# Depthwise convolution of a two-layer decoder step: four channel chunks on TensorE in sixteen 32x32 pieces, four on VectorE with prompt and sample taps in turn

## The reference, cut to what matters

```python
def conv_glu(h, w_pw1, b_pw1):
    u = h @ w_pw1 + b_pw1
    a, g = jnp.split(u, 2, axis=-1)
    return a * jax.nn.sigmoid(g)

def conv_rest(u_ext, w_dw, b_dw, ln_g, ln_b, w_pw2, b_pw2):
    c = lax.conv_general_dilated(u_ext, w_dw[:, None, :], window_strides=(1,), padding='VALID',
                                 dimension_numbers=('NWC', 'WIO', 'NWC'),
                                 feature_group_count=D_CONV) + b_dw
    c = layernorm(c, ln_g, ln_b)
    return jax.nn.silu(c) @ w_pw2 + b_pw2
```

## Time and profile before

| | us |
|---|---|
| median of three runs | 2173.63 (2168.54 to 2174.45) |
| profiled execution, its own time | 2175.05 |
| its span in the trace | 2173.3 |
| first product starts (L1968) | 1257.4 |
| last gate (gate 7) starts | 1442.7 |
| diagonal matmuls end | 1475.4 |
| second product starts | 1500.5 |
| expert layer 1 starts its matmuls | 1632.8 |

### The profile page before, as it was taken

The page is one execution under the profiler, slowest core; times in us unless marked ns, Lnnn a source line. Parts: engine busy times, 40 slices in busy tenths (PEclk is TensorE's granted clock), DMA queues, the critical chain, the costliest instruction groups (busy, mean ns, idle before and its releaser), DMA issues.

```text
span 2173.3 us, 32073 instructions
## 1 busy us (share of the span) xinstructions
PE 1667.7 (77%) x12540; PEld 806.9 (37%) x12540; DVE 688.0 (32%) x1216; ACT 303.1 (14%) x716; POOL 291.4 (13%) x416
## 2 busy tenths in 40 slices
PE   4999888887885778778777296768849778887770
PEld 2444455554445222223223174544443222222220
DVE  3214477767215100000000369983160000000003
ACT  1000344343210000000000100003101000000001
POOL 1001113212100100000000065400010000000001
PEclk9999989898895899999999698889959989889995
DMA  9476389889821699999999589902308999999973
GB/s 360 149 270 223 130 304 345 320 330 338 342 111 49 253 427 429 427 416 428 422 417 421 195 296 328 320 11 116 132 32 331 427 426 424 422 426 426 428 333 144
DMA packets 98431, 659.02 MB, mean 303 GB/s; under 512 B 14939, under 2 KB 14940, under 8 KB 69498
## 3 DMA queue, kind: packets, MB, share of 16 engines
q1 hardware_dynamic: 67450, 557.96, 64.1%
q0 software_dynamic: 30864, 99.45, 12.5%
HBM read 643.07 MB, written 96.53 MB: 340 GB/s over the span
## 4 chain that ended last, share of the span: by engine, by line
PE 42%; DMA 35%; DVE 16%; issue 4%; ACT 2%; SPq 1%; POOL 0%; DVEq 0%; POOLq 0%; ACTq 0%
DMA ring<-in 32%; PE ps L1861 13%; PE ps L1548 9%; DVE big L1446 7%; PE ps L1823 6%; PE ps L1505 3%; PE ps L1667 2%; PE ps L1989 1%; DVE ring L1052 1%; DMA big<-y_rows 1%; PE ps L1877 1%; PE ps L1607 1%; PE ps L1652 1%; PE ps L1583 1%; PE ps L1968 1%
## 5 line engine op out<-in xcount | busy, mean ns | idle before, releaser
L1861 PE MATMUL ps<-ring,big 128*32 128x512 f32 (+1 forms) x2816 | 511.7, 657 | 153.2 <-DMA ring<-in 150.4
L1861 PEld LDWEIGHTS ps<-ring,big 128*32 128x32 f32 (+1 forms) x2816 | 161.0, 133 | 502.9 <-issue 431.1
L1246 DVE TENSOR_TENSOR big<-big,ps 128x512 f32<-128x512 f32 x32 | 22.0, 687 | 892.3 <-PE ps L1861 892.3
L1877 PE MATMUL ps<-ring,big 128*32 128x512 f32 (+1 forms) x1408 | 230.0, 602 | 37.9 <-ACT big L634 23.0
L1548 PE MATMUL ps<-ring,act_t 128*128 128x512 f32 (+1 forms) x480 | 189.5, 594 | 1.2 <-DVEq L320 1.2
L634 ACT ACTIVATE big<-ps 128x512 f32<-128x512 f32 (+2 forms) x128 | 71.3, 557 | 748.5 <-PE ps L1505 433.7
L1505 PE MATMUL ps<-cst,big 128*128 128x128 f32 (+2 forms) x552 | 85.9, 310 | 109.2 <-DVE big L1019 68.8
L1968 PE MATMUL ps<-act_t,ring 128*128 128x288 f32 x512 | 133.1, 424 | 36.5 <-DVE big L1431 35.3
L1446 DVE SCALAR_TENSOR_TENSOR big<-big,par 128x512 f32<-128x512 f32 x150 | 152.3, 1015 | 5.1
L1877 PEld LDWEIGHTS ps<-ring,big 128*32 128x32 f32 (+1 forms) x1408 | 72.7, 123 | 172.8 <-issue 172.8
L1823 PE MATMUL ps<-ring,big 128*128 128x512 f32 (+1 forms) x288 | 121.7, 608 | 8.0 <-ACT big L954 7.1
(11 more groups left out here) (262 smaller groups left out, 1497.5 us busy)
## 6 DMA issues: line engine op xcount, KB each, us to landing
ring<-in SPq DMA_DIRECT2D x206, 2048.0 KB, 19.3
out<-in SPq DMA_DIRECT2D x16, 4080.0 KB
ring<-in SPq DMA_DIRECT2D x128, 256.0 KB, 7.8
ring<-in POOLq DMA_DIRECT2D x128, 256.0 KB, 8.4
ring<-in SPq DMA_DIRECT2D x24, 512.0 KB, 5.3
ring<-in POOLq DMA_DIRECT2D x24, 512.0 KB, 4.5
ring<-in SPq DMA_DIRECT2D x8, 1024.0 KB, 8.7
ring<-in POOLq DMA_DIRECT2D x8, 1024.0 KB, 7.7
```

The lines of the kernel that those rows point to most:

```text
L1246: V.tensor_tensor(hb, sg, ps[:, 1, :], ALU.mult).then_inc(m["hb"], 1)
L1861: ins = mm(ps[half, i, :], XgT[:, par_, k, half], slot(eslots(w)[i], 8)[:, k, :], start=(k == 0), stop=(k == KC - 1))
L1877: ins = mm(ps[half, 5 + h, :], hbT[:, k, half], slot(eslots(w)[2], 4)[:, k, h * 512:(h + 1) * 512], start=(k == 0), stop=(k == 3))
```

## The change

- TensorE takes four chunks (4 to 7) in sixteen pieces a step; VectorE takes chunks 0 to 3.
- VectorE does each prompt tap and the same tap of the 64 sample columns in turn; each waits for the one two places back, that is for the one before of its own kind. The samples of chunks 4 to 7 are done by `sample_taps`.
- GpSimd does no taps and no diagonals: VectorE builds the diagonals ahead of gate 0, in slot 1.
- The gates stand at other places. The turned samples and products move to slot 2.
- `w_pw2` goes to slots 0 and 3. Slot 0 is loaded at once behind `w_pw1`; slot 3 after chunk 3, and the window copies stand behind that wait. The experts' first loads go in the order 5, 2, 4, 1, 0, 3.
- Reciprocal, scaling and Silu are done for 288 columns of all chunks and then for the other 288; `project` waits for the second half at its third unit.

The core of the diff:

```diff
     def moe_base(l, s):
-        return 16 + (16 if s in (2, 3) else 0) + l * (16 * NPB + 16)
+        return 16 + (16 if s in (2, 3) else 0) + l * (16 * NPB + 16 + {1: -16, 3: 16}.get(s, 0))
...
-    D_CH = KC - 3
-    diag = slot(2, 128)
-    fresh = ring[:, 3, 0:KC * TS].rearrange("p (c q) -> p c q", c=KC)
+    D_CH = KC - 4
+    diag = slot(1, 128)
+    fresh = ring[:, 2, 0:KC * TS].rearrange("p (c q) -> p c q", c=KC)
...
-            for s in ((5, 4, 0, 2, 3, 1) if l == 0 else (2, 5, 3, 0, 4, 1)):
+            for s in ((5, 4, 0, 2, 3, 1) if l == 0 else (5, 2, 4, 1, 0, 3)):
...
-                    if s < 2:
-                        sp.wait_ge(p_mm, len(P_UNITS) + (5, len(P_UNITS))[s])
+                    if s in (0, 3):
+                        sp.wait_ge(p_mm, len(P_UNITS) + (5 if s == 0 else len(P_UNITS)))
+                    elif s == 2:
+                        sp.wait_ge(pw_mm, KC + 1)
+                        sp.wait_ge(ln_steps, 1)
                     else:
-
-                        sp.wait_ge(pw_mm, KC + 2 if s == 2 else KC)
-                        if s == 3:
-                            sp.wait_ge(ln_steps, 1)
+                        sp.wait_ge(pw_mm, KC + 2 if s == 1 else KC)
...
-        sp.wait_ge(pw_mm, 1)
-        for n in range(2):
-            sp.dma_start(slot(n, 8), w2[n]).then_inc(loaded[n], 16)
+        sp.dma_start(slot(0, 8), w2[0]).then_inc(loaded[0], 16)
+        sp.wait_ge(pw_mm, 4)
+        sp.dma_start(slot(3, 8), w2[1]).then_inc(loaded[3], 16)
         for i in range(6, 2 * NB):
             copy_window(i)
...
         for ch in range(KC):
             act.wait_ge(ln_steps, KC + 4 + ch)
-            A_(cc[:, ch, :], cc[:, ch, :], ACT.Silu, bias=PR("ln_b")[:, ch:ch + 1],
+            A_(cc[:, ch, 0:HALF], cc[:, ch, 0:HALF], ACT.Silu, bias=PR("ln_b")[:, ch:ch + 1],
                scale=PR("ln_g")[:, ch:ch + 1]).then_inc(ln_squares, 1)
+        for ch in range(KC):
+            act.wait_ge(ln_steps, 2 * KC + 4 + ch)
+            ins = A_(cc[:, ch, HALF:], cc[:, ch, HALF:], ACT.Silu, bias=PR("ln_b")[:, ch:ch + 1],
+                     scale=PR("ln_g")[:, ch:ch + 1])
+        ins.then_inc(ln_squares, 1)
...
-            o = cc[:, ch, 0:TP]
             for j in range(CK):
                 if j in gates:
                     gate(gates[j])
-                i = u_ext[:, ch, j:j + TP]
-                if j == 0:
-                    link(V.tensor_scalar(o, i, wdw[:, ch, 0:1], PR("b_dw")[:, ch:ch + 1], ALU.mult, ALU.add))
-                else:
-                    link(V.scalar_tensor_tensor(o, i, wdw[:, ch, j:j + 1], o, ALU.mult, ALU.add))
+                for o, i in ((cc[:, ch, 0:TP], u_ext[:, ch, j:j + TP]), (sample_sums(ch), us[:, ch, :, j:j + NQ])):
+                    if j == 0:
+                        S(V.tensor_scalar(o, i, wdw[:, ch, 0:1], PR("b_dw")[:, ch:ch + 1], ALU.mult, ALU.add))
+                    else:
+                        dve.wait_ge(dve_step, S.n - (3 if j in gates else 1))
+                        S(V.scalar_tensor_tensor(o, i, wdw[:, ch, j:j + 1], o, ALU.mult, ALU.add))
...
+        for a in range(4):
+            V.tensor_tensor(diag[:, 32 * a:32 * a + CK, :], C("eye32").unsqueeze(1).broadcast_to((P, CK, 32)),
+                            wdw[:, D_CH + a, :].unsqueeze(2).broadcast_to((P, CK, 32)), ALU.mult)
+        for a in range(4):
+            ins = V.tensor_tensor(diag[:, 32 * a + CK, :], C("eye32"),
+                                  PR("b_dw")[:, D_CH + a:D_CH + a + 1].broadcast_to((P, 32)), ALU.mult)
+        ins.then_inc(diagonals, 1)
         gate(0)
-        taps(0, {22: 1})
-        taps(1, {13: 2})
-        taps(2, {4: 3, 26: 4})
-        taps(3, {17: 5})
-        taps(4, {8: 6, 30: 7})
+        taps(0, {16: 1})
+        taps(1, {2: 2, 20: 3})
+        taps(2, {4: 4, 22: 5})
+        taps(3, {6: 6, 24: 7})
...
-        link(V.reciprocal(inv, inv))
-        for ch in range(KC):
-            V.tensor_tensor(cc[:, ch], cc[:, ch], inv, ALU.mult).then_inc(ln_steps, 1)
+        for h in range(2):
+            part = slice(h * HALF, (h + 1) * HALF)
+            link(V.reciprocal(inv[:, part], inv[:, part]))
+            for ch in range(KC):
+                V.tensor_tensor(cc[:, ch, part], cc[:, ch, part], inv[:, part], ALU.mult).then_inc(ln_steps, 1)
...
-        pe.wait_ge(diagonals, 1)
+        pe.wait_ge(diagonals, 2)
         for j in range(CK + 1):
             for g in range(4):
                 p = slice(32 * g, 32 * g + 32)
-                for a in range(3):
+                for a in range(4):
...
-            G(nc.gpsimd.tensor_tensor(xx, xx, bias_rows[0:rows(t), :], ALU.add))
-        G.done()
-
-        def sample_taps(ch):
...
+            ins = nc.gpsimd.tensor_tensor(xx, xx, bias_rows[0:rows(t), :], ALU.add)
         ins.then_inc(diagonals, 1)
```

More of the change, by code:

```diff
@@ L461, in tap_products @@
         return flat.rearrange("p (b q j) -> p b q j", b=NB, q=NQ)
-    pool_taps, dve_taps = tap_products(B(12528, NTAP)), tap_products(ring[:, 3, 512:512 + NTAP])
+    dve_taps = tap_products(ring[:, 2, 512:512 + NTAP])
     def sample_operands(ch):
@@ L1454, in sample_taps @@
             return V.tensor_scalar(cc[:, ch, TP:T], cc[:, ch, TP:T], PR("b_dw")[:, ch:ch + 1], None, ALU.add)
-        gate(0)
-        taps(0, {22: 1})
-        taps(1, {13: 2})
-        taps(2, {4: 3, 26: 4})
-        taps(3, {17: 5})
-        taps(4, {8: 6, 30: 7})
+        for a in range(4):
[5 more added lines that the diff above has]
+        ins.then_inc(diagonals, 1)
+        gate(0)
+        taps(0, {16: 1})
+        taps(1, {2: 2, 20: 3})
+        taps(2, {4: 4, 22: 5})
+        taps(3, {6: 6, 24: 7})
         dve.wait_ge(pw_mm, 4)
-        S(sample_taps(D_CH))
-        S(sample_taps(D_CH + 1))
-        sample_taps(D_CH + 2).then_inc(ln_steps, 1)
+        for ch in range(D_CH, KC - 1):
+            S(sample_taps(ch))
+        sample_taps(KC - 1).then_inc(ln_steps, 1)
         dve.wait_ge(pw_mm, KC + 2)
-        for a in range(3):
+        for a in range(4):
             for g in range(2, 4):
@@ L1479, in _ @@
         dve.wait_ge(ln_squares, KC + 2)
-        link(V.reciprocal(inv, inv))
-        for ch in range(KC):
-            V.tensor_tensor(cc[:, ch], cc[:, ch], inv, ALU.mult).then_inc(ln_steps, 1)
+        for h in range(2):
[3 more added lines that the diff above has]
+                V.tensor_tensor(cc[:, ch, part], cc[:, ch, part], inv[:, part], ALU.mult).then_inc(ln_steps, 1)
+        dve.wait_ge(diagonals, 2)
         residual(1)
@@ L1804, in _, with project @@
         fence()
-        def project(u, lhs, first, done, between=None, chunk_ready=None):
+        def project(u, lhs, slots_, done, between=None, chunk_ready=None):
             for i, unit in enumerate(P_UNITS):
@@ L1811, in project @@
                     if t in (0, 4):
-                        pe.wait_ge(loaded[first + n], done[n])
+                        pe.wait_ge(loaded[slots_[n]], done[n])
                 if i >= 4:
@@ L1819, in project @@
                 for k in range(KC):
-                    if i == 0 and chunk_ready:
-                        chunk_ready(k)
+                    if chunk_ready and (i == 0 or (i, k) == (2, 0)):
+                        chunk_ready(i, k)
                     for j, (n, t) in enumerate(unit):
-                        ins = mm(ps[unit_rows(t, j), i % 4, :], lhs(k, t), slot(first + n, 8)[:, k, :],
+                        ins = mm(ps[unit_rows(t, j), i % 4, :], lhs(k, t), slot(slots_[n], 8)[:, k, :],
                                  start=(k == 0), stop=(k == KC - 1))
@@ L1834, in finish_rows @@
             ins.then_inc(f_mm, 1)
-        project(0, mixed, 2, [moe_base(0, s) for s in (2, 3)], finish_rows)
+        project(0, mixed, (2, 3), [moe_base(0, s) for s in (2, 3)], finish_rows)
         fence()
@@ L1961, in _ @@
                 for s in (first, first + 1):
-                    pe.wait_ge(loaded[s], moe_base(1, s))
+                    pe.wait_ge(loaded[s], moe_base(1, s) - (16 if s == 3 else 0))
             if ch > 1:
@@ L1994, in _ @@
         pe.wait_ge(ln_steps, 1)
-        pe.wait_ge(diagonals, 2)
         for ch in range(KC):
@@ L2008, in _ @@
             ins.then_inc(ln_sums, 1)
-        project(1, lambda k, t: cc[:, k, t * P:t * P + rows(t)], 0, [moe_base(1, s) for s in range(2)],
-                chunk_ready=lambda k: pe.wait_ge(ln_squares, KC + 3 + k))
+        project(1, lambda k, t: cc[:, k, t * P:t * P + rows(t)], (0, 3), [moe_base(1, s) for s in (0, 3)],
+                chunk_ready=lambda i, k: pe.wait_ge(ln_squares, KC + 3 + (k if i == 0 else KC)))
         fence()
@@ L2200, in _ @@
             xx = xt[0:rows(t), t, :]
-            G(nc.gpsimd.tensor_tensor(xx, xx, bias_rows[0:rows(t), :], ALU.add))
-        G.done()
-        def sample_taps(ch):
[L2206 to L2228, removed]
+            ins = nc.gpsimd.tensor_tensor(xx, xx, bias_rows[0:rows(t), :], ALU.add)
         ins.then_inc(diagonals, 1)
-        G(sample_taps(3))
-        G.done()
```

(1 more changed line is left out.)

## The result

Over 17 runs each the changed kernel takes 2159.1 us in the median (2145.0 to 2165.1) and the kernel before 2170.0 (2161.2 to 2179.9). The ratio is 0.9938, interval 0.9919 to 0.9957. The forecast was 2118, a gain of 2.6%; the gain is 0.6%, and 2159.1 lies outside the range of 2109 to 2140.

The account below looks back on a forecast made before the run. VectorE's queue of taps was taken to set gate 7, and gate 7 the rest. Terms -54.8 + 1.5 - 2.4 = -55.7 us took the profiled 2175.05 to 2119.4, hence a median of 2118; range 2109 to 2140.

Parts of the forecast that it names:

- What bounds the kernel: Convolution stage: VectorE's queue, 161.7 of 185.3 us busy, sets when gate 7 comes, and gate 7 the rest.
- front: Ahead of gate 0: VectorE's diagonal builds collide with GpSimd's bias adds; gate 0 at 1280.4, bounds 1276 and 1282.5.
- a pair of taps: VectorE's prompt tap plus its sample tap overlap and cost 0.86 us, against 1.10 if each waits.
- to gate 7: VectorE from gate 0: seven gates and 117 pairs, gate 7 at 1387.9, a gain of 54.8 us.
- Diagonal matmuls: TensorE behind gate 7: sixteen pieces cost a step no more than twelve, 0 us; the stage keeps 30.83 us.
- Rival (b): Diagonal matmuls: sixteen pieces are slower than twelve, 9 us more, 2127; chance 0.07.
- Queues: DMA queues: window copies held behind chunk 3 run to 1459, experts' loads to 1484, needed at 1577; nothing else waits.
- (d): Rival, expert layer: copies and loads reach into it and give back the convolution's saving, nothing gained; chance 0.02.
- Copies out of PSUM: Behind the diagonal matmuls: eight copies, 5.5 us, against four chunks' sums, 4.0; +1.5 us on the path.
- norm: Before the second product: halved reciprocal saves 1.88 us, scaling 0.3, Silu 0.2; together -2.4, second half hidden.
- behind gate 7 on VectorE: Seven pairs and four sample chunks, done at 1414, hidden under diagonal matmuls ending at 1420.6.

Follow-up runs that it names:

- e10: e4 with VectorE's diagonals built ahead of the wait for the state rows; 2132.0 us, ratio 0.9822.
- e12: e4 with both edits, diagonals built ahead of the state wait and the last two copies behind the experts' four loads; 2119.3 us, ratio 0.9772.
- e1: Changed kernel without ten of the sixteen window copies; 2128.1 us, ratio 0.9808.
- e5: Changed kernel with its ten copies each cut into 510 rows of 8 KB in place of 16 rows of 255 KB; 2156.3 us, ratio 0.9932.
- e9: Changed kernel with its ten copies in pieces of 8 KB that cannot be joined; 2141.2 us, ratio 0.9851.
- e11: e4 with eight copies behind chunk 0 and the last two behind the experts' four loads; 2118.4 us, ratio 0.9754.
- e4: Changed kernel with copies issued after chunk 0 as before, experts' first loads held until the diagonal matmuls are done; 2127.5 us, ratio 0.9794.
- e3: Kernel before with its copies held until chunk 7's product ends, to run under its twelve-piece diagonal matmuls; 2190.1 us, ratio 1.0087.
- e7: e4 with the two inner loops of the diagonal matmuls exchanged, so neighbouring pieces use different row groups; 2132.2 us, ratio 0.9828.
- e8: Changed kernel with only the copies, slot 3's load behind them, moved back to chunk 0's end; experts' loads as changed; 2140.0 us, ratio 0.9836.
- e6: e4 with four of the ten copies issued in layer 0, behind the first loads of its experts; 2165.5 us, ratio 0.9973.

## Why the prediction was wrong

- *What bounds the kernel*, *front*, *a pair of taps*, *to gate 7*: right. Gate 0 at 1280.75 for 1280.4, a pair 0.86, gate 7 at 1387.4 for 1387.9. The pair settles the weighing: by the sentence of the Trainium skill, "VectorE: DVE Perf Modes", section "The DRAIN you can't avoid", that leaving out semaphores saves nothing, the pair was to cost 1.10; the trace shows 0.86 where the wait is already satisfied. That *front* came out within 0.4 us was partly luck: the state landed at 1273.96, not 1270.4, and only the first of the four builds met an add (3.16 us; the others took 1.18). e10, which builds ahead of the wait, shows the price of building behind it: gate 0 comes 18.0 us after the first product's start for 24.6, and 5.1 us of that are left at gate 7.
- *Diagonal matmuls* failed, twice. "The fourth column group rides along: 0 us": it costs 5 us (e12 against a twelve-piece step). I read two entries 0.86 apart in rows 9 as a rate; they are starts of weight loads, one step apart. The row of their matmuls, which I left out, has 128 records in 5.90 us, 1.48 a step, a little over half of it at 1.2 GHz:

```profile
504.81 5.90 PE L1667 MATMUL ps<-ring 32*16 32x512 f32 x128
```

  Rival (b) named the effect and put 9 us on it; 5 were measured, and its reason, four pieces reading the same rows, is not shown. And "the stage keeps its 30.83" took for granted that its surroundings stay.
- *Queues* is the step that failed for good. It moved the copies by 46 us, worked out that they run to 1459 (they ended near 1455), and then asked only who waits for their data: "Nothing else waits". The stage from 1388 to 1420 lay wholly under them, and TensorE's own instructions come over the same engines. The cost: 60.8 less the clean 33.3 is 27.5 us. 15.5 are the stops. About 3 are the half clock at the start, which the kernel before had too and the prediction counted on; e1 has it without the copies. The remaining 9, an estimate by difference, are the half clock behind the stops. So of the 29.9 us that the stage grew, 5 are the fourth column group and about 25 the transfers over it. No rival named it; (d) had the copies collide with the experts instead.
- *Copies out of PSUM* +1.9 for 1.5, *norm* -2.3 for -2.4, *behind gate 7 on VectorE*: right. From the diagonal matmuls' end to the second product's start 24.7 us stand where 25.1 stood.
- Not foreseen: in this execution norm and routing ahead of the experts took 76.4 us instead of 67.9, with a granted clock of 0.60 in the window of the norm against 0.82 before; the experts and the rest took 4.9 less. It is not tied to one version: profiles of e5 to e9 and e11 have 76.4 or 76.5, those of before, e1 to e4, e10 and e12 67.5 to 67.9. That it changes from one execution of a kernel to the next is likely but not shown, as each was profiled once; e11's profiled execution took 2129.5 us where four others took 2117.6 to 2118.5 and a fifth 2136.7. Why it falls one way or the other stays open.
- Against the forecast of 2119.4 for the profiled execution, 2153.3 is 34 us more: 29.9 the stage, 8.6 norm and routing, -4.9 the experts and the rest, and 0.4 the second product. The median lies another 6 above that.

## What to carry to other kernels

When a transfer is moved, ask what it will lie under, not only who needs its data: this stage of short matmuls used a 16 KB block of instructions every 4 us, and busy DMA engines turned that into stops. Read the instruction queue's line in the DMA view of such a stage; "issue" gaps at equal counts of records are its sign. Keep bulk copies and prefetches out of that stretch, before it or behind it, and take a rate from a long row, never from two neighbours.

## What the runs showed of the hardware

- TensorE's fetch: one 16 KB packet per 128 records with their weight loads. Beside copies the bursts start 7.3 to 9.8 us apart, with 8 KB packets 6.2 to 7.3, each less than 3 us behind a packet of its own (changed kernel). On nearly idle engines there is no stop at 4.0 us per block (e12).
- The first stop stands behind 283 records (changed kernel, e3, e7, e9) or already behind 155, 128 fewer (e4, e5, e8, e10).
- 32x32 pieces of 512 columns at full clock: 35.6 ns a record with twelve, 30.4 to 31.6 with sixteen.
- Behind a wait for gate 7 of 5.0 to 5.1 us, TensorE ran the first 4 to 5 us of the stage at 1.2 GHz (changed kernel, e1, e11); behind one of 3.3 us (e6), and in e12, without such a wait, at 2.4 GHz throughout.
- GpSimd's row stores on the software queue were waited for 25 and 33 us beside four window copies (e6).
- 510 rows of 8 KB that lie one behind the other travelled in packets of 53 KB, 16 rows of 255 KB in packets of 51 KB (e5, changed kernel); cut out of order, in packets of 8.0 KB (e9).
